# ScalarE's own DMA queue for the stores at the end of the mixer blocks, in a one-core encoder step

## The reference

```
z = rmsnorm(x, norm1) @ w_in                      # 3088 columns, split into seven parts
y = concat(rmsnorm(bg * causal_dwconv(cg * h)), rmsnorm(gla(q, k, v, gate)) * silu(r)) @ w_out
x = x + y                                         # "the mixers' rows"
xn = rmsnorm(x, norm2)                            # "the second norm's rows"
u = causal_dwconv(xn @ w_up); a, g = split(u)     # 2 x 2816 columns
x = x + (silu(g) * a) @ w_down
return rmsnorm(x, final_norm), the new states
```

## Time and profile before

| | before |
|---|---|
| median of 3 runs (lowest, highest) | 2442.91 us (2440.92, 2445.68) |
| profiled execution, its time | 2440.73 us |
| profiled execution, span of its instructions | 2439.0 us |
| PE busy | 2329.7 us, 96% |
| DVE, ACT, POOL busy | 66%, 40%, 48% |
| stores of the mixers' rows (L692) | 17 |
| stores of the second norm's rows (L701) | 9 |

### The profile page before, as it was taken

The page is one execution under the profiler, slowest core; times in us unless marked ns, Lnnn a source line. Parts: engine busy times, 40 slices in busy tenths (PEclk is TensorE's granted clock), DMA queues, the critical chain, the costliest instruction groups (busy, mean ns, idle before and its releaser), DMA issues. The chain is left out here.

```text
span 2439.0 us, 39246 instructions
## 1 busy us (share of the span) xinstructions
PE 2329.7 (96%) x13090; PEld 2127.6 (87%) x13090; DVE 1602.0 (66%) x2415; ACT 974.4 (40%) x1879; POOL 1161.3 (48%) x1125
## 2 busy tenths in 40 slices
PE   7999999999999998599999999999999998999996
PEld 6899878899788986599999998899999997999995
DVE  2046671155650667599889888676676677878787
ACT  4333353333453434344444445433333345344443
POOL 3222323222523336687787786444444454555552
PEclk9999999999999999799999999999999999999998
DMA  5111335111452233744444446644444466555552
GB/s 163 52 52 44 121 113 177 44 52 44 143 187 76 72 121 133 270 175 155 167 160 155 169 158 248 240 142 150 156 142 151 154 211 233 194 193 198 193 196 78
DMA packets 260718, 358.59 MB, mean 147 GB/s; under 512 B 12284, under 2 KB 198481, under 8 KB 260625
## 3 DMA queue, kind: packets, MB, share of 16 engines
q1 hardware_dynamic: 260625, 357.33, 43.5%
HBM read 278.32 MB, written 78.97 MB: 146 GB/s over the span
## 5 line engine op out<-in xcount | busy, mean ns | idle before, releaser
L1374 PE MATMUL ps<-xo,wq 128*128 128x384 f32 (+1 forms) x1848 | 599.7, 325 | 41.7 <-DVE xo L1726 17.1
L1375 PE MATMUL ps<-xo,wq 128*128 128x384 f32 (+1 forms) x1848 | 598.6, 324 | 0.0
L1376 PE MATMUL ps<-xo,wq 128*128 128x384 f32 (+1 forms) x1848 | 598.3, 324 | 0.0
L1979 DVE TENSOR_TENSOR resid<-resid,ps 128x512 f32<-128x512 f32 (+1 forms) x748 | 489.9, 680 | 74.7 <-PE ps L1376 46.1
L471 POOL TENSOR_TENSOR w_lo<-raw,w_hi 128x512 fp32r<-128x512 f32 x192 | 251.1, 1334 | 575.4 <-ACT w_hi L464 575.4
L872 POOL TENSOR_TENSOR wq<-wu_raw,wq 128x256 fp32r<-128x256 f32 x396 | 384.7, 995 | 94.1 <-ACT wq L982 94.1
L1374 PEld LDWEIGHTS ps<-xo,wq 128*128 128x128 f32 x1848 | 350.6, 190 | 63.3 <-issue 36.4
L1375 PEld LDWEIGHTS ps<-xo,wq 128*128 128x128 f32 x1848 | 351.2, 190 | 20.3
L1376 PEld LDWEIGHTS ps<-xo,wq 128*128 128x128 f32 x1848 | 351.2, 190 | 0.0
L1374 PE MATMUL ps<-xt_hi,w_hi 128*128 128x384 f32 (+4 forms) x960 | 316.5, 330 | 6.4 <-DVE xt_lo L1718 3.3
L1996 DVE SCALAR_TENSOR_TENSOR up_y<-up_u,params,up_y 128x768 f32<-128x768 f32 (+1 forms) x264 | 287.2, 1088 | 49.5 <-ACT up_y L1018 30.8
(11 more groups left out here) (197 smaller groups left out, 3537.5 us busy)
## 6 DMA issues: line engine op xcount, KB each, us to landing
wq<-w_ops SPq DMA_DIRECT2D x176, 512.0 KB, 4.5
wu_raw<-in_w_up_dram SPq DMA_DIRECT2D x89, 512.0 KB, 4.0
w_ops<-wq SPq DMA_DIRECT2D x88, 512.0 KB, 2.7
raw<-in_w_in_dram SPq DMA_DIRECT2D x72, 512.0 KB, 3.8
wd_raw<-in_w_down_dram SPq DMA_DIRECT2D x66, 512.0 KB, 5.3
x_in<-in_x_prompt_dram SPq DMA_DIRECT2D x32, 512.0 KB, 4.4
raw<-in_w_out_dram SPq DMA_DIRECT2D x24, 512.0 KB, 3.3
wu_raw<-in_w_up_dram SPq DMA_DIRECT2D x43, 256.0 KB, 2.9
```

Source lines behind the costliest of these rows:

```text
L1374: pe.matmul(out, lh, rh, start=(first and n == 0), stop=False, skip_group_check=skip)
L1375: pe.matmul(out, ll, rh, start=False, stop=False, skip_group_check=skip)
L1376: last = pe.matmul(out, lh, rl, start=False, stop=end, skip_group_check=skip)
L1979: last = dve.tensor_tensor(resid[0:m, t, s], resid[0:m, t, s], ps[0:m, bank, :], ALU.add)
```

## The change

The 17 stores of the mixers' rows and the 9 stores of the second norm's rows leave SP's stream and enter ACT's. The first stand between ACT's wait for `out_read` and `norm_rstd`; the second come after the last `norm_copy` of a block, behind a wait for ACT's own copies. The stores of the sums and all loads stay with SP. DVE gets a wait for the nine second stores before it writes `r_3`, which lies in the same memory as a part of their sources, in the first FFN step.

```diff
@@ SP
                     if b + 1 < NB and NX + j < TILES[b + 1]:
                         first[b + 1].wait(sp, "scaled", j + 1)
                         load_x(NX + j, b + 1)
-                    mix.wait(sp, "out_read", 6 * nt + 2 * (j + 1))
-                    m = tile_cols(b, t)[1]
-                    sp.dma_start(mid_rows(b, t), resid[0:m, t, :]).then_inc(mid_stored, 16)
 
                 if b == NB - 1:
                     mix.wait(sp, "out_done", 8 * nt)
                     n2.wait(sp, "squared", nt)
                     for i in range(3, 5):
                         load_x_op(0, i)
-                n2.wait(sp, "hi", 2 * nt)
-                for i, half, c0 in ((0, 0, 0), (2, 1, 0), (6, 1, c)):
-                    sp.dma_start(x_ops[b, i, :, :, 0:c], stash(b, half)[:, :, c0:c0 + c]).then_inc(ops_stored, 16)
                 if b == NB - 1:
                     sp.wait_ge(wu_lo, splits(0, 0, 5))
                     load_up(0, 1)
@@ ACT
                         n2.wait(act, "scaled", j - 1)
                         mix.wait(act, "out_read", 6 * nt + 2 * (j + 1))
+                        act.dma_start(mid_rows(b, order[j]), resid[0:m, order[j], :]).then_inc(mid_stored, 16)
                         norm_rstd(n2, j, m, resid[0:m, order[j], :], junk[0:m, :])
@@ ACT
                     if j >= 2:
                         norm_copy(n2, j - 2, b, order[j - 2], (stash(b, 0), stash(b, 1)))
+                    if j == nt + 1:
+                        n2.wait(act, "hi", 2 * nt)
+                        if b == NB - 1:
+                            act.wait_ge(gap_zero, 8)
+                        h = HALF[b]
+                        for i, half, c0 in ((0, 0, 0), (2, 1, 0), (6, 1, h)):
+                            act.dma_start(x_ops[b, i, :, :, 0:h], stash(b, half)[:, :, c0:c0 + h]).then_inc(ops_stored, 16)
@@ DVE
                 dve.wait_ge(up_done, NP * g + 4)
+                if edge == 0 and b == 0:
+                    dve.wait_ge(ops_stored, 16 * 3 * NB)
                 dve.tensor_tensor(r_3[:, 0:h], ps[:, 1, 0:h], r_1[:, 0:h], ALU.add).then_inc(r3_read, 1)
```

## The result

The changed kernel takes 2445.15 us (median of 22 runs, 2443.98 to 2449.45) and the kernel before 2442.16 us (22 runs, 2438.86 to 2446.19). The ratio is 1.0016, 95% interval 1.0009 to 1.0022: slower by 3.9 us (2.2 to 5.4), clearly not zero. The ratio itself lies within the 0.2% (4.9 us) that the prediction counts as "same"; the end of its interval does not. One run of experiment 6's kernel took 2904.74 us at a mean granted clock of 0.75 and is left out of every comparison. The profiled execution took 2444.83 us with a span of 2443.1 us, against 2440.73 and 2439.0 before.

A forecast was written before the change was run, and what follows sets the result against it. PE bounds most of the span, a ring through DVE and ACT the last passes of blocks 0 and 1. Terms 3.5 + 0 + 0.8 + 0 = 4.3 us on 2442.91 gave 2447.2 us, range for 8 in 10 2442.5 to 2452.5.

The forecast's parts named there:

- The ring: Last pass of blocks 0 and 1: add (DVE), Square, root, copy (ACT), subtraction, scaling, next add (DVE), 6.00 us a tile.
- the price of a first store: Between ACT's wait for `out_read` and the Square: 0.35 us each, five a block in blocks 0 and 1, 3.5 us.
- Second stores in blocks 0 and 1: Three stores ahead of ACT's table load, covered because PE needs ACT's read only later: cost 0.
- Second stores in block 2: ACT's fourth high part comes later, so POOL, SP's loads and PE's restart follow 0.8 us later; bounds 0.35 and 1.9.
- PE's wait of 17.1 us: End of block 2, PE waiting for DVE's low part; the prediction called itself wrong if this wait shrinks.
- What SP gains: SP loses 26 stores and the waits ahead of them, but had slack already: worth nothing.
- DVE's wait and the queue: DVE's new wait before `r_3` finds the stores landed, and bytes and DMA engines are the same: cost and gain 0.
- Nearly free: Rival, chance 0.20: each store's issue on ACT takes some 0.05 us, 0.7 us in all, 2443.6 us.
- Costs more: Rival, chance 0.27: each of ten first stores on ACT costs 0.58 us, 8.2 us in all, 2451.1 us.
- faster transfers: Rival, chance 0.05: a second queue speeds transfers at the end of block 2 by 4.6 us, giving 2439.0 us.

The follow-up runs named there:

- experiment 6: Kernel before, all stores on SP, with ACT's copy for the next block moved ahead of the Square: 2430.40 us against 2441.88, ratio 0.9954.
- experiment 2: Kernel before with only the 17 first stores moved to ACT, second stores on SP: 2445.76 us against 2441.85, ratio 1.0018.
- experiment 3: Kernel before with only the first stores moved to ACT, each issued at the end of its tile's turn: 2440.8 us against 2441.85, ratio 0.9994.
- experiment 1: Kernel before with only the nine second stores moved to ACT, first stores on SP: 2441.72 us against 2441.85, ratio 1.0001.
- experiment 5: Kernel before with the second stores moved to ACT, each followed by a copy of itself to a spare buffer: 2455.44 us against 2441.88, ratio 1.0057.
- experiment 7: Changed kernel with ACT's copy for the next block moved ahead of the Square: 2431.53 us against 2441.88 for the kernel before, ratio 0.9961.
- experiment 4: Changed kernel with a 64 KB store to a spare buffer behind each first store: 2451.8 us against 2441.85 for the kernel before, ratio 1.0049.

## Why the prediction was right

- **The ring and the price of a first store.** Forecast 0.35 us for each of ten, 3.5 us, Squares 6.35 apart. Measured 0.37, 6.37 apart, 1.84 and 1.82 us in blocks 1 and 0, 3.7 together; experiment 2 gives +3.9 for these stores alone, 3 shows that outside the ring they are free, and 6 that the ring did set the pace. Right in mechanism and size, the size with some luck: SP's row gave 0.31, and "a little over" had no row behind it. The 0.06 that SP's row lacks lies in the start: SP's store began 0.03 us after the add's end (345.08), where ACT's begins 0.09 after it (346.24 to 346.33).
- **Second stores in blocks 0 and 1.** Forecast 0, by cover. Measured 14.18 against 14.19 us in block 1, and experiment 1 is level with before. Experiment 5 shows that it is cover. The forecast of 0.9 us in block 1 for each issue half a microsecond dearer left out the clock: a PE wait there costs more than its length (5.9 us for 3.8 in experiment 5).
- **Second stores in block 2.** Forecast 0.8 us, measured 0.1 (0.16 in experiment 1), within the scatter of that stretch. This is the term that was mis-sized, under its lower bound of 0.35. The high part and POOL were late about as computed: POOL starts the pair 0.96 us later against the pass, where 0.82 was forecast. The step that failed is that POOL's later subtractions keep their length. The two pairs that took 5.81 us took 1.63 and 3.23, and `low_x` 7.08 for 7.45, which takes up the 0.35 us of the first store. Both return in the other traces: the two pairs take 5.80 or 5.81 us together in the kernel before and in experiments 2, 3 and 6, with the second stores on SP, and 4.85 to 4.91 in the changed kernel and in experiments 1 and 7, with them on ACT. `low_x` takes 7.08 in the changed kernel and in experiments 2 and 7, where the first stores stand ahead of the Square, and 7.45 to 7.47 in the other four. Why the pairs get shorter is argued only. DVE, too, waits for ACT there and is idle from 972.6 to 973.6, where it worked without a break before. In the kernel before, a pair at 998.27 that falls wholly in a pause of DVE takes 1.41 us. And it holds the other way round: DVE's last sum (L1932, at 971.95) takes 0.69 us while POOL waits, and took 1.11 before while POOL worked. So the two engines seem to slow each other when both work, and a delay that lets them take turns gives most of itself back; no run tried this by itself.
- **A sign that came although the mechanism held.** The prediction called itself wrong if PE's wait of 17.1 us shrinks, and it did, to 16.4. But so it did in experiment 3 (16.5), where neither kind of store delays the ring or the block's end. The wait is a difference of two times: PE came to it 0.8 us later in the changed kernel, and its restart was not earlier but 0.10 us later. The sign should have been the restart against the pass's start.
- **What SP gains.** Forecast nothing. Experiments 1 and 3 take one or the other kind of store from SP and neither is faster beyond its interval.
- **DVE's wait and the queue.** Forecast nothing; in experiments 1 and 3, which carry the wait, no loss shows.
- **The sum.** 4.3 us forecast. The pieces measured in the profile are 3.7 + 0.1 = 3.8; the ratio says 3.9 us (2.2 to 5.4), the medians 3.0. The profiled executions differ by 4.1, but that is not a closer check: 0.4 of it lies before the first block's pass, another 0.4 between blocks 1 and 2, and 0.5 is given back in the FFN, all in stretches where the two kernels are the same. The forecast time, 2447.2, is 2 us above the measured 2445.15; 0.75 of that is that the kernel before came out at 2442.16 in 22 runs and not at the 2442.91 of three.
- **The rivals.** "Nearly free" is wrong at the place where the change puts the stores and right elsewhere: beside work that runs already ACT does not feel them (experiment 7, and in block 2 two of the changed kernel's own stores stand under a copy of 1.49 us). "Costs more" did not come about with one store a tile; with two, single stores were held for 1.3 and 1.7 us (experiment 4). Nothing spoke for faster transfers: from `load_up(0, 1)` to `load_down(0)` it is 16.68 us before (975.23 to 991.91) and after (979.99 to 996.67). The Trainium skill's rule that more issuing engines save only the sequencer's issue time (DMA: Bandwidth & Descriptors, "Issuing engines are not separate DMA queues") agrees with experiments 1 and 3 (2441.72 and 2440.80 us against 2441.85).

## What to carry to other kernels

An issue of a DMA has a price for the engine that makes it, here 0.33 us for 512 KB, and whether it is paid depends on what stands ahead of it in that engine's stream: behind a wait for the same event that releases the next piece of the critical ring it is paid in full, each time; beside running work, in the idle time before another wait, or on an engine that does not set the pace, it is free. So before moving issues to another engine, find the ring that sets the pace and put the issue at a point outside it; and look at the ring first, since an order of ACT's stream that took the Square out of it gave -11 us, three times what the stores' place was worth. And a delay followed through a chain of engines need not arrive whole: here 0.8 us at POOL were 0.26 at SP's load, because POOL's instructions behind it got shorter.

## What the runs showed of the hardware that was not expected

- A store of 16 partitions and 64 KB, right behind another store, held ACT for 0.45 us (443 to 1735 ns over 17), one of 128 partitions and 512 KB for 0.33.
- Three stores of 768 KB in a row held ACT for 2.7 us, six for 7.4 (experiment 5); from the third on each took 1.4 to 1.7 us, the first two 0.5 to 0.7.
- A DMA's issue on ACT runs beside ACTIVATEs that stand ahead of it in the stream, and can start before the last of them (343.65, with copies at 343.43 and 343.91, experiment 7).
- Two pairs of POOL's subtractions took 5.81 us beside a DVE at work and 4.86 where DVE was idle for 0.97 us of them; DVE's sum beside them took 1.11 and 0.69 us. That the one causes the other was not tried by itself.
- A PE wait of 2.7 us was followed by five microseconds at a granted clock of 0.50 and cost 5.85 us in all (experiment 5).
